# A stick-breaking attention stage rewritten as 32 unrolled steps with both heads of a pair side by side

## The reference, cut to what matters

```
q, k, v, gate = split(h @ w_in, 4)
q = rms_norm(q per head, q_norm_g); k = rms_norm(k per head, k_norm_g)
z      = q @ k^T / 8                                 # per head, 512 x 512
mask   = key_pos < query_pos
log1m  = where(mask, -softplus(z), 0)
after  = reverse_cumsum(log1m over keys) - log1m
wts    = where(mask, exp(log_sigmoid(z) + after), 0)
o      = wts @ v
out    = (o * silu(gate)) @ w_out
```

## Time and profile before

| what | us |
|---|---|
| median of three runs | 1987.3 |
| the profiled execution, whole | 1985.26 |
| its span, first to last instruction | 1983.5 |
| PE matmul busy | 1857.0 (94%) |
| DVE busy | 937.3 (47%) |
| ACT busy | 838.9 (42%) |
| POOL busy | 614.8 (31%) |

### The profile page before, as it was taken

How to read it: one execution, slowest core, us unless ns; L and a number is a source line. 1 busy time by engine, 2 the same in 40 slices (tenths; PEclk the granted TensorE clock), 3 DMA queues, 4 the chain that set the end, 5 groups by cost and what they waited for, 6 DMA issues and landing times.

```text
span 1983.5 us, 23150 instructions
## 1 busy us (share of the span) xinstructions
PE 1857.0 (94%) x8864; PEld 1488.8 (75%) x8864; DVE 937.3 (47%) x1306; ACT 838.9 (42%) x1191; POOL 614.8 (31%) x154
## 2 busy tenths in 40 slices
PE   5999768899998999999999999999999987899999
PEld 4688658778888566658878888888767866787787
DVE  6665944355123343443564433431376595344610
ACT  5574223377232565663332222222357523236821
POOL 3333211034442101112434444434423222012342
PEclk9999879999999999999999999999999987999999
DMA  4223120022222101011222323232321312001222
GB/s 167 76 74 107 56 62 12 1 85 86 100 92 85 43 22 42 21 43 64 89 89 99 105 86 106 85 106 85 106 81 69 98 66 75 12 6 45 104 93 77
DMA packets 46977, 144.66 MB, mean 73 GB/s; under 512 B 28080, under 2 KB 28208, under 8 KB 30768
## 3 DMA queue, kind: packets, MB, share of 16 engines
q1 hardware_dynamic: 46896, 143.55, 21.7%
HBM read 138.29 MB, written 5.24 MB: 72 GB/s over the span
## 4 chain that ended last, share of the span: by engine, by line
PE 76%; DVE 15%; ACT 5%; issue 2%; DMA 1%; SPq 0%; POOL 0%; DVEq 0%; ACTq 0%
PE ps L1461 18%; PE ps L1463 18%; PE ps L1462 18%; DVE acc L986 3%; PE ps L1700 3%; DVE tmp L1119 3%; PE ps L1882 2%; PE ps L1920 2%; DVE acc L989 2%; PE ps L1908 1%; PE ps L1753 1%; DVE hf L928 1%; PE ps L1739 1%; PE ps L1710 1%; PE ps L1726 1%
## 5 line engine op out<-in xcount | busy, mean ns | idle before, releaser
L385 POOL TENSOR_TENSOR w_lo<-w_raw,w_hi 128x2048 fp32r<-128x2048 f32 x126 | 588.6, 4671 | 1116.8 <-ACT w_hi L453 1116.8
L1461 PE MATMUL ps<-h_hi,w_hi 128*128 128x512 f32 x1488 | 604.7, 406 | 55.3 <-POOL w_lo L385 27.5
L1462 PE MATMUL ps<-h_lo,w_hi 128*128 128x512 f32 x1488 | 587.6, 395 | 0.0
L1463 PE MATMUL ps<-h_hi,w_lo 128*128 128x512 f32 x1488 | 587.1, 395 | 0.0
L1461 PEld LDWEIGHTS ps<-h_hi,w_hi 128*128 128x128 f32 x1488 | 284.9, 191 | 129.6 <-issue 40.3
L1462 PEld LDWEIGHTS ps<-h_lo,w_hi 128*128 128x128 f32 x1488 | 284.6, 191 | 62.6 <-issue 4.8
L1463 PEld LDWEIGHTS ps<-h_hi,w_lo 128*128 128x128 f32 x1488 | 284.2, 191 | 60.9
L453 ACT ACTIVATE w_hi<-w_raw 128x2048 fp32r<-128x2048 f32 x126 | 240.2, 1906 | 129.1 <-PE ps L1463 123.4
L1461 PE MATMUL ps<-y_hi,w_hi 128*128 128x512 f32 x448 | 174.3, 389 | 0.0
L1463 PE MATMUL ps<-y_hi,w_lo 128*128 128x512 f32 x448 | 174.3, 389 | 0.0
L1462 PE MATMUL ps<-y_lo,w_hi 128*128 128x512 f32 x448 | 174.3, 389 | 0.0
(11 more groups left out here) (181 smaller groups left out, 2385.1 us busy)
## 6 DMA issues: line engine op xcount, KB each, us to landing
w_raw<-w_tiles SPq DMA_DIRECT2D x126, 1024.0 KB, 4.9
x<-x_t SPq DMA_DIRECT2D x4, 512.0 KB, 9.1
out_t<-x SPq DMA_DIRECT2D x8, 256.0 KB, 5.4
scr_u<-lt SPq DMA_DIRECT2D x8, 128.0 KB, 2.7
u_blk<-scr_u SPq DMA_DIRECT2D x2, 512.0 KB, 3.3
scr_v<-v_blk SPq DMA_DIRECT2D x2, 512.0 KB, 2.6
scr_t<-v_t SPq DMA_DIRECT2D x2, 512.0 KB, 3.6
d_g<-scr_t SPq DMA_DIRECT2D x32, 32.0 KB, 2.0
```

The lines of the kernel that those rows point to most:

```text
L385: pool.tensor_tensor(w_lo[:, slot, :], w_raw[:, slot, :], w_hi[:, slot, :].bitcast(F32), ALU.subtract).then_inc(lo_done, 1)
L1461: pe.matmul(out_, w_h, m_h, start=start, stop=False)
L1462: pe.matmul(out_, w_h, m_l, start=False, stop=False)
L1463: return pe.matmul(out_, w_l, m_h, start=False, stop=stop)
```

## The change: what it does

The eight units of a pair become four steps; 32 steps g = 4j + v (pair j, v = 0 to 3, width 128(v+1)) stand unrolled, with no loop. A step takes both heads: z of both heads one after the other into two banks of two alternating couples (`z_bank`: banks 2, 3 or 4, 5), then both masks; 2 blocks; one sum of squares for v = 1 and 3; pv of step g-2 for both heads; 1 block; cum of step g-1 for both; 1 block. z(g) waits for the weights of step g-2.

The blocks are one stream of 144: pair 0's own 16 and 8 of pair 1's tile ahead of the first step, then 4 in every step until the first gate tile (t0+12) is done too, which happens in step v = 1 of pair 7. The bank function is shifted by one from tile t0+12 on, since the gate tile now goes to banks 0 and 1. `gate_step` leaves the first tile out on PE.

On ACT a step is abs, abs, exp, exp, ln, ln, then a square (v = 0, 2) or a reciprocal root (v = 1, 3) for the next pair, then both weights of step g-1, and at v = 2 `hi(t0+7+j)`. On DVE a step is the copy of one projected half (v = 0, 2), then softplus, high and low part of head 0 and of head 1, then for v = 1 and 3 the scaling of one half of the next pair. DVE also makes the low part of tiles t0+7 to t0+13 (`low_w`) at v = 0, in place of POOL, which makes tiles up to t0+6 and from t0+14 on.

```diff
@@ -256,7 +256,9 @@
     def bank(s, c):
-        return ps[2 * (s % 2) + c]
+        return ps[2 * ((s + (s >= turn)) % 2) + c]
+    turn = tile_base[layers.index(SB)] + 12
...
+    def z_bank(g, e):
+        return ps[2 + 2 * (g % 2) + e]
...
@@ -422,6 +427,12 @@
                         clear(d, c + 1)
                     decay_q(d, c, 1)
                 lows(tile_base[l] + 18, TILES[kind] - 18)
+            elif kind == SB:
+                t0 = tile_base[l]
+                lows(t0, 7)
+                pool.wait_ge(lo_done, t0 + 14)
+                pool.wait_ge(b["spl"], 6 * SB_PAIRS)
+                lows(t0 + 14, TILES[kind] - 14)
             else:
                 lows(tile_base[l], TILES[kind])
...
+            def softplus(g):
+                w = P * (g % 4 + 1)
+                for e in range(2):
+                    act.wait_ge(b["z"], 2 * g + e + 1)
+                    if g:
+                        act.wait_ge(b["sp"], 2 * g + e - 1)
+                    act.activation(sb_t[:, e, 0:w], z_bank(g, e)[:, 0:w], ACT.Abs).then_inc(b["abs"], 1)
+                for e in range(2):
+                    act.wait_ge(b["abs"], 2 * g + e + 1)
+                    act.activation(sb_t[:, e, 0:w], sb_t[:, e, 0:w], ACT.Exp, scale=-1.0).then_inc(b["exp"], 1)
+                for e in range(2):
+                    act.wait_ge(b["exp"], 2 * g + e + 1)
+                    act.activation(sb_t[:, e, 0:w], sb_t[:, e, 0:w], ACT.Ln, bias=1.0).then_inc(b["ln1"], 1)
+            def weights(g):
+                w = P * (g % 4 + 1)
+                for e in range(2):
+                    act.wait_ge(b["cum"], 2 * g + e + 1)
+                    if g:
+                        act.wait_ge(b["pv"], 2 * g + e - 1)
+                    act.activation(sb_w[:, e, 0:w], z_bank(g, e)[:, 0:w], ACT.Exp).then_inc(b["w"], 1)
             hi(t0 + 5)
...
+            square_qk(0, 0)
+            square_qk(0, 1)
+            hi(t0 + 6)
+            rms_qk(0, 0)
+            rms_qk(0, 1)
+            for j in range(SB_PAIRS):
+                more = j + 1 < SB_PAIRS
+                for v in range(4):
+                    g = 4 * j + v
+                    softplus(g)
+                    if more and v in (0, 2):
+                        square_qk(j + 1, v // 2)
+                    if more and v in (1, 3):
+                        rms_qk(j + 1, v // 2)
+                    if g:
+                        weights(g - 1)
+                    if v == 2:
+                        hi(t0 + 7 + j)
+            weights(4 * SB_PAIRS - 1)
...
+            def scaled_qk(p, c):
+                gain = par[:, c0["k"]:c0["k"] + 1] if c else gq8[:, 0:1]
+                dve.wait_ge(b["r"], 2 * p + c + 1)
+                dve.wait_ge(b["raw"], 2 * p + c + 1)
+                if p == 0 and c == 0:
+                    dve.wait_ge(b["gq8"], 1)
+                if p >= 2:
+                    dve.wait_ge(b["z"], 8 * (p - 1))
+                dve.scalar_tensor_tensor(sb_qk[:, p % 2, c, :], sb_raw[:, c, :], gain, sb_r[:, c, :],
+                                         ALU.mult, ALU.mult).then_inc(b["qk"], 1)
+            def values(p):
+                if p >= 2:
+                    dve.wait_ge(b["pv"], 8 * (p - 1))
+                dve.tensor_copy(sb_v[:, p % 2, :, :], v_tok[:, :, p * P:p * P + P]).then_inc(b["v"], 1)
+            def softplus(g):
+                j, v = g // 4, g % 4
+                w = P * (v + 1)
+                off = (0, 128, 384, 768)[v]
+                for e in range(2):
+                    dve.wait_ge(b["ln1"], 2 * g + e + 1)
+                    if v == 0 and j:
+                        dve.wait_ge(b["cum"], 2 * g + e - 1)
+                    dve.scalar_tensor_tensor(sb_sp[:, e, off:off + w], z_bank(g, e)[:, 0:w], 0.0,
+                                             sb_t[:, e, 0:w], ALU.max, ALU.add).then_inc(b["sp"], 1)
+                    if v:
+                        to = slice(off - P, off - P + w)
+                        dve.wait_ge(b["sp"], 2 * g + e + 1)
+                        dve.tensor_copy(sp_hi[:, e, to], sb_sp[:, e, off:off + w]).then_inc(b["sph"], 1)
+                        n = 6 * j + 2 * (v - 1) + e
+                        dve.wait_ge(b["sph"], n + 1)
+                        dve.tensor_tensor(sp_lo[:, e, to], sb_sp[:, e, off:off + w], sp_hi[:, e, to].bitcast(F32),
+                                          ALU.subtract).then_inc(b["spl"], 1)
+            def low_w(t):
+                dve.wait_ge(hi_done, t + 1)
+                dve.wait_ge(lo_done, t)
+                dve.tensor_tensor(w_lo[:, t % 2, :], w_raw[:, t % 2, :], w_hi[:, t % 2, :].bitcast(F32), ALU.subtract)\
+                    .then_inc(lo_done, 1)
+            def evac(j):
+                dve.wait_ge(b["pv"], 8 * (j + 1))
+                dve.tensor_copy(o_sb[:, j, :], ps[6 + j % 2][:, :]).then_inc(b["ev"], 1)
...
+            raw_qk(0, 0)
+            raw_qk(0, 1)
+            scaled_qk(0, 0)
+            scaled_qk(0, 1)
+            values(0)
+            for j in range(SB_PAIRS):
+                more = j + 1 < SB_PAIRS
+                for v in range(4):
+                    if more and v in (0, 2):
+                        raw_qk(j + 1, v // 2)
+                    softplus(4 * j + v)
+                    if v == 0 and j:
+                        low_w(t0 + 6 + j)
+                    if more and v in (1, 3):
+                        scaled_qk(j + 1, v // 2)
+                    if v == 2 and j:
+                        evac(j - 1)
+                    if v == 2 and more:
+                        values(j + 1)
+            evac(SB_PAIRS - 1)
...
+            def project(n):
+                t, c, k = t0 + 4 + n // 16, n // 8 % 2, n % 8
+                if k == 0:
+                    if c == 0:
+                        pe.wait_ge(lo_done, t + 1)
+                    pe.wait_ge(proj_free, 2 * (t0 + 4) if n < 16 else 2 * (t - 1) + c + 1)
                 mm = in_block(t, c, k, bk=ps[c])
                 if k == KD - 1:
                     mm.then_inc(proj_done, 1)
...
+            def sums(p, c):
+                pe.wait_ge(b["sq"], 2 * p + c + 1)
+                pe.wait_ge(b["raw"], 2 * p + c + 1)
+                pe.matmul(ps[c][:, :], cf[:, C_BLOCK:C_BLOCK + P], sb_sq[:, c, :], start=True, stop=True).then_inc(b["ss"], 1)
+            def z(g):
+                j, kb = g // 4, 3 - g % 4
+                w = T - P * kb
                 if kb == 3:
...
-            def pair(j, i, first, last):
-                t = t0 + 4 + j
-                rest = list(parts)
-                for u in range(8):
-                    z(u, j, i)
-                    if not last:
-                        if u == 0:
-                            qk_ready(t + 1, i)
-                        if u < len(share):
-                            for _ in range(share[u]):
-                                qk_part(t + 1, i, *rest.pop(0))
-                    if not (first and u < 2):
-                        cum(8 * j + u - 2, i)
-                    if not (first and u < 3):
-                        pv(8 * j + u - 3, i)
-                    if u == 5 and not last:
-                        sums(j + 1, i)
-            pair(0, 0, True, False)
...
+            def cum(g):
+                j, v = g // 4, g % 4
+                w = P * (v + 1)
+                for e in range(2):
+                    bk = z_bank(g, e)
+                    if v == 0:
+                        pe.wait_ge(b["sp"], 2 * g + e + 1)
+                    else:
+                        if g == 1:
+                            pe.wait_ge(b["tri"], 1)
+                        pe.wait_ge(b["spl"], 6 * j + 2 * (v - 1) + e + 1)
+                    for v2 in range(v, -1, -1):
+                        w2 = P * (v2 + 1)
+                        off = (0, 128, 384, 768)[v2]
+                        c = 0 if v2 == v else P
+                        if v2 == 0:
+                            mm = pe.matmul(bk[:, w - w2:w], cf[:, C_TRI + c:C_TRI + c + P], sb_sp[:, e, 0:w2],
+                                           start=False, stop=True, skip_group_check=True)
+                            continue
+                        for part in (sp_hi, sp_lo):
+                            pe.matmul(bk[:, w - w2:w], tri_r[:, c:c + P], part[:, e, off - P:off - P + w2],
+                                      start=False, stop=False, skip_group_check=True)
+                    mm.then_inc(b["cum"], 1)
+            def pv(g):
+                j, kb = g // 4, 3 - g % 4
+                w = T - P * kb
+                pe.wait_ge(b["w"], 2 * g + 2)
+                if kb == 3:
+                    pe.wait_ge(b["v"], j + 1)
+                    if j >= 2:
+                        pe.wait_ge(b["ev"], j - 1)
+                for e in range(2):
+                    own = slice(64 * e, 64 * e + 64)
+                    pe.matmul(ps[6 + j % 2][own, kb * P:T], sb_v[:, j % 2, kb, own], sb_w[:, e, 0:w],
```

(73 more changed lines are left out.)

116 lines of the change are left out of this document (23 added, 93 removed).

## The result

| | before | after |
|---|---|---|
| median | 1986.0 us (4 runs, 1983.9 to 1988.5) | 1950.5 us (4 runs, 1949.6 to 1952.3) |
| the profiled execution | 1985.3 | 1952.3 |

The ratio is 0.9822, 95% interval 0.9805 to 0.9839. The prediction was 1965 us with a range of 1956 to 1983; the result is the figure of its rival "full overlap" (1950, chance 0.06).

What follows compares the result with a forecast made beforehand. PE's own issue was taken to bound pairs 1 to 6. Changes of -1 (through pair 0), -15 (pairs 1 to 6) and -6.7 (pair 7, gate tile) took 1985.3 to 1962.6; median 2.0 higher: 1965 us, range 1956 to 1983.

Steps and rivals of the forecast that it cites:

- full overlap: Rival for z and pv: the second head's streaming lies entirely under the first's; 26.9 us a pair, 1950 us; chance 0.06.
- the overlap: z and pv of the two heads: one pass in four overlaps, saving 1.07 us each per pair; chance 0.57.
- Where PE bounds, and the fixed parts: PE's issue bounds pairs 1 to 6; a pair's 31.47 us holds 26.5 of work and 4.6 of fixed parts.
- The new wait: Step v=3: the next pair's z waits for DVE's scaling after all softplus operations; 8.9 us against 8.0 of PE work.
- Ahead of pair 0 and pair 0: From the first sums of squares to pair 1: -1 us, most idle stays, no half clock assumed, worth 1.5 us.
- Pair 7 and the gate tile: Pair 7 and first gate tile, blocks in the first two steps only: 30.1 us instead of 36.8, -6.7.
- serial sum: Pair 7 and first gate tile if the heads follow each other: 32.7 us, -4; chance of serial heads 0.28.
- Low parts on DVE: Step v=0: at most 2.8 us of low parts on DVE, covered by its free time, so no cost.
- The clock: Rival: idle before each new pair's z halves the clock, 12 us in all; chance 0.09 shared with an unfilled last pair.

Runs made afterwards that it cites:

- runs with one half: Changed kernel with head 1 computing in head 0's half of the array: z only 1967.8 us, pv only 1964.3 us, z and pv 1979.1 us.
- serial run: Changed kernel with both z and pv of head 1 put in head 0's half of the array; 1979.1 us, a pair 30.87 us.
- head 1 narrow: Changed kernel, but where z is 512 columns wide, head 1's z makes only its first 128 columns; 1952.1 us.

## Why the prediction was wrong

*The step that failed* is the overlap. The prediction bounded z and pv from both sides, 2.13 us a pair each for a full overlap, and took half of that, because "the two passes of a head need new weights in the same half, so they can't overlap, and matmuls start in order". The passes of one head do follow each other (0.53 us apart). But head 1 does not wait for them: its first pass starts 0.007 us after head 0's first, not with head 0's second at 0.53. So the term was 2.13 us a pair where the runs with one half show 3.7 (30.9 against 27.2). The streaming that overlaps is 4.27, and the idle in front of the next pair, 0.52 in that run and 1.08 in the changed kernel, takes back the other 0.6. The full-overlap rival had 26.9 us a pair and 1950 in all; 27.2 and 1950.5 were measured. (Its 26.9 has a slip: step v=1 is 6.2 by the prediction's own terms, not 6.0, and 6.19 was measured; the 0.1 added to the other cases is left out too.) Its chance of 0.06 was the mistake, and with it the low end at 1956: a bound that no row excludes got next to nothing because of an argument on order that no row supported either.

*Where PE bounds, and the fixed parts*: right. The serial run has the predicted steps within 0.15 us.

*The new wait*: right. The chain for step v=3 was put at 8.5 us with full overlap and took 8.53. The idle stands in front of each pair and is released by DVE's scaling, and moving the scaling away gave 7.4 us.

*Ahead of pair 0 and pair 0*: -1.9 where -1 was put; pair 0 took 22.4 us instead of 23.4, the overlap again. Block 17 waits for the first ln behind ACT's rounding as described (653.27, 1.25 us idle). That no half clock followed, as assumed, is luck: with the same two idles ahead of pair 0, 0.58 and 1.25 us, the clock fell to half behind them in four of the other nine traces, the runs with z in one half, with both in one half, with 128 blocks and with head 1 narrow, and pair 0's first z came 1.6 us later there (11.2 us after the first sum of squares instead of 9.6). And the k half was scaled at 658.5, not as early as put (651.7): the scaling of the q half, 0.75 us otherwise, took 4.05 beside POOL's 4.61. The eight blocks covered it, with 0.4 us to spare.

*Pair 7 and the gate tile*: -9.0 for -6.7, the difference again the overlap. In the run with both in one half this part took 32.4 us, and the prediction's serial sum was 32.7.

*Low parts on DVE*: their cost was nothing, as put: each took 2.28 us, and step v=0 took 7.07 where the sum without them was 7.0. What they save was missed: the prediction compared two places for the work by the room there, not by what POOL's instruction does to DVE's.

*The clock*: the 1.08 us of idle in front of each pair left it alone, as the prediction held; 2.33 us brought it down behind four of seven.

## What to carry to other kernels

Two float32 matmuls on different halves of the array that stand next to each other cost here as much as one, and a mask over the whole array between them undid it. When pairs of small matmuls are put side by side, the engines behind them can become the chain: see what the first instruction of the next group waits for, and move that piece of work between the halves of the current one. Before a term is set between two bounds, ask which row speaks for the middle; if none does, the ends need real chances.

## What the runs showed of the hardware that I had not expected

- The two passes of a float32 matmul on one half of the array run on without regard to the other half: starts 0, 0.007, 0.220, 0.534 us with 512 columns on one half and 128 on the other.
- A DVE rounding from SBUF to SBUF (0.43 us) that met a 4.59 us subtraction on POOL took 1.67 us and ended 0.29 us after it, while a DVE operation with a PSUM operand in the same stretch kept its 0.69. A scaling from SBUF to SBUF (0.75) took 4.05 beside such a subtraction and ended 0.54 us after it.
- The same idles did not always have the same effect on the clock. In the last pair of the changed kernel, idles of PE of 1.61 and 1.85 us passed at a granted clock of 1.00; in the run with head 1 narrow, idles of 1.61 and 1.87 in the same places were followed by half clock from 866.0. Which other condition decides is open.
